# Part of a depthwise convolution moved from the Vector engine to the Scalar engine and GpSimd, in a one-core hybrid block (convolution, differential attention, mixture of experts)

## The chip, the core and the metric

The kernel runs on one NeuronCore of a Trainium2 chip, in one launch. The metric is the device time of one execution in microseconds (us). Engines are named as the profile names them: PE (matmuls), PEld (its weight loads), DVE (Vector engine), ACT (Scalar engine), POOL (GpSimd), SP (issues DMAs).

## What is computed

512 tokens of width 1024, float32. One layer: RMS norm, a projection to five groups of 512 columns (a, g, q, k, v), a convolution branch on a and g, an attention branch on q, k and v, an output projection of both, then 32 experts with the best four for each token. The branch that the change touches:

```python
def conv_mixer(a, g, conv_w, conv_b, ln_g, ln_b):
    u = a * jax.nn.sigmoid(g)
    y = lax.conv_general_dilated(u, kern, window_strides=(1,),
                                 padding=[(CONV_WIDTH - 1, 0)],      # CONV_WIDTH = 31, causal
                                 dimension_numbers=('NWC', 'WIO', 'NWC'),
                                 feature_group_count=D_CONV)        # 512 channels, one filter each
    y = layer_norm(y + conv_b, ln_g, ln_b)
    return jax.nn.silu(y)
```

The attention branch has 4 heads with two softmaxes each, `p[:, :, 0] - lam * p[:, :, 1]`, over blocks of 128 queries; `lam` is a scalar computed with two exponentials.

## The kernel before, in words

All matmuls of float32 data are done as three matmuls of a split: `hi` is the value rounded to fp32r, `lo` the rest. ACT makes `whi` of each chunk of weights, DVE makes `wlo` (`hi_front` and `lo_front` in the front part). The front part has 14 chunks of weights, numbered 0 to 13: two for each of a, g, q, k, v (0 to 9) and four of the output projection. PE takes chunk c once `lo_front(c)` is done, 48 matmuls each; `hi_front(c)` waits until PE has used chunk c - 3, because there are three `whi` buffers.

Each engine has its order of work written out by hand. DVE's, from the end of the second group (g):

1. `u_pad = a * sigmoid(g)`, signalled by `conv_in`.
2. `lo_front(6)`, 20 taps, `lo_front(7)`, 20 taps, `lo_front(8)`, 18 taps, scaling of q, `lo_front(9)`, 18 taps, `lo_front(10)`, 16 taps, scaling of k, `lo_front(11)`, four evictions of the transposed k (`kT`).
3. Three small instructions for `lam` (they wait for ACT's exponential, `lam_exp`), and then 16 attention units (4 query blocks x 4 heads). For unit i DVE takes the row maxima of unit i + 1, forms the difference `pd` of the two softmaxes of unit i, and then does 6 taps (units 0 to 4) and the remaining 2 (unit 5).

The convolution has 4 channel groups c of 128 channels, with 31 taps w each: 124 taps. A tap is one instruction on [128, 512]: it multiplies a shifted window of `u_pad` by a weight of its own for each partition and adds it to `acc`. The first tap of a group is a TENSOR_SCALAR (L849), the other 30 are SCALAR_TENSOR_TENSORs (L853). Each waits on a semaphore for the tap before it of the same group. The taps of two groups alternate (2 and 0, then 3 and 1), so that two taps in a row never depend on each other.

PE, ACT and DVE then do the layer norm between attention units: the mean is four fp32 products of `inv_dc` and `acc` (L1235), one for each channel group (group 2 in unit 3, group 0 in unit 4, groups 3 and 1 in unit 5); DVE's subtraction of the mean (`centre`, L914) follows in unit 6.

ACT in the same stretch: `hi_front(6)`, `hi_front(7)`, `hi_front(8)`, the evictions and squares of q (`qk_out(0)`, 4 evictions and 32 squares), `hi_front(9)`, `hi_front(10)`, the same for k (`qk_out(1)`), `hi_front(11)`, evictions of transposed q (`qT`, L597) and of v (`v_tok`, L600), the exponential for `lam` (L601), then the exponentials of the units. PE transposes q inside chunk 9 and k behind it (`turn_qk`, L1172); the first waits for the squares of both q and k, the second for DVE's scaled `k_tok` and for ACT's `qT`.

POOL has no work between its setup at the start and the end of attention. In the expert loop behind it POOL gathers tokens, scatters results by indirect DMA, and moves four columns of indices with four small copies per iteration (L480 to L485), while DVE subtracts `whi` from the weights (L1049) all the time.

## Time and profile before

| what | value |
|---|---|
| median of 3 runs | 1544.02 us (1540.77 to 1546.91) |
| the profiled execution's own time | 1540.77 us |
| its span in the profile | 1539.2 us |
| mean granted TensorE clock | 0.957 of full speed |
| busy: PE, DVE, ACT, POOL | 95%, 86%, 65%, 17% |

The span runs from the first to the last instruction in the trace. The front part (projections, attention, output projection, routing) lies between 0 and about 340 us; the expert loop takes the rest. The change touches the stretch from 70 to 200 us alone. A busy share over the whole span says little on that stretch, so its own rows are what to look at.

### The profile page before, as it was taken

To read this page: it belongs to the slowest core of one execution; us is meant where nothing else is said; L and a number is where in the kernel's file an instruction comes from. 1 tells how busy PE (TensorE), PEld (TensorE's weight loads), DVE (VectorE), ACT (ScalarE), POOL (GpSimd) and SP (SyncE) were. 2 spreads that over 40 slices of the span, in tenths; PEclk is the share of its full clock that TensorE was granted. 3 is DMA by queue.
4 is the path that set the end of the run, shared out by engine and by line. 5 is a ranking of instruction groups with operands and counts; after the bars stand their busy time and mean duration, and the time that the engine had idled before them with its cause. 6 is when DMAs were issued, how large, how long until landed. Compare 5 with 4: busy or idle time off the path is not lost.

```text
span 1539.2 us, 19983 instructions
## 1 busy us (share of the span) xinstructions
PE 1456.7 (95%) x6488; PEld 1160.2 (75%) x6488; DVE 1319.1 (86%) x1082; ACT 1005.0 (65%) x942; POOL 263.2 (17%) x277
## 2 busy tenths in 40 slices
PE   7996899929999999999999999999999999999996
PEld 5885457817888888888888888888888888887884
DVE  3499866547999999999999999999999999999994
ACT  5353264326777777777777777777777777777773
POOL 2000000230111221112211111122111212212121
PEclk9998589859999999999999999999999999999998
DMA  8330003677999999999999999999999999999971
GB/s 289 114 108 2 1 1 135 223 124 290 343 348 377 361 364 356 355 363 361 356 352 357 363 353 359 362 347 358 360 345 361 366 347 358 362 356 356 353 265 20
DMA packets 94743, 445.31 MB, mean 289 GB/s; under 512 B 14879, under 2 KB 14895, under 8 KB 61888
## 3 DMA queue, kind: packets, MB, share of 16 engines
q1 hardware_dynamic: 80704, 421.82, 73.9%
q0 software_dynamic: 11392, 17.61, 4.9%
q10 hardware_dynamic: 2624, 5.59, 1.4%
q8 instruction: 13, 0.21, 0.1%
q14 instruction: 10, 0.08, 0.0%
HBM read 439.56 MB, written 22.43 MB: 300 GB/s over the span
## 4 chain that ended last, share of the span: by engine, by line
PE 86%; DVE 9%; DMA 2%; issue 1%; ACT 1%; POOL 1%; ACTq 0%; POOLq 0%; DVEq 0%
PE psum L1148 25%; PE psum L1149 25%; PE psum L1150 25%; DVE acc L853 5%; PE psum L1417 2%; PE psum L1392 2%; PE psum L1401 2%; PE psum L1434 1%; PE psum L1220 1%; DVE wlo L808 1%; DMA slot_table<-payload,dest 1%; PE psum L1280 1%; POOL slot_table L441 0%; PE psum L1155 0%; PE psum L1222 0%
## 5 line engine op out<-in xcount | busy, mean ns | idle before, releaser
L1049 DVE TENSOR_TENSOR wlo<-ring,whi 128x2048 fp32r<-128x2048 f32 x384 | 876.7, 2290 | 80.6 <-ACT whi L719 77.0
L719 ACT ACTIVATE whi<-ring 128x2048 fp32r<-128x2048 f32 x384 | 737.9, 1922 | 275.4 <-PE psum L1150 275.4
L1148 PE MATMUL psum<-whi,xT_hi 128*128 128x512 f32 x1024 | 406.5, 397 | 4.0 <-DVE xT_lo L1055 4.0
L1149 PE MATMUL psum<-whi,xT_lo 128*128 128x512 f32 x1024 | 400.4, 391 | 0.0
L1150 PE MATMUL psum<-wlo,xT_hi 128*128 128x512 f32 x1024 | 400.0, 391 | 0.0
L1148 PEld LDWEIGHTS psum<-whi,xT_hi 128*128 128x128 f32 x1024 | 193.3, 189 | 53.9 <-issue 10.9
L1150 PEld LDWEIGHTS psum<-wlo,xT_hi 128*128 128x128 f32 x1024 | 193.2, 189 | 40.7
L1149 PEld LDWEIGHTS psum<-whi,xT_lo 128*128 128x128 f32 x1024 | 193.4, 189 | 38.0
L1148 PE MATMUL psum<-whi,aT_hi 128*128 128x512 f32 x512 | 202.5, 396 | 1.9 <-ACT y_sb L741 1.9
L1149 PE MATMUL psum<-whi,aT_lo 128*128 128x512 f32 x512 | 200.2, 391 | 0.0
L1150 PE MATMUL psum<-wlo,aT_hi 128*128 128x512 f32 x512 | 200.2, 391 | 0.0
L468 POOL DMA_INDIRECT out<-y_sb,slots x32 | 98.5, 3078 | 419.6 <-ACT y_sb L741 405.7
L1148 PEld LDWEIGHTS psum<-whi,aT_hi 128*128 128x128 f32 x512 | 96.6, 189 | 21.3 <-issue 2.2
L1150 PEld LDWEIGHTS psum<-wlo,aT_hi 128*128 128x128 f32 x512 | 96.5, 189 | 20.2
L1149 PEld LDWEIGHTS psum<-whi,aT_lo 128*128 128x128 f32 x512 | 96.5, 189 | 19.3
L853 DVE SCALAR_TENSOR_TENSOR acc<-u_pad,cw_sb,acc 128x512 f32<-128x512 f32 x120 | 80.5, 752 | 0.0
L480 POOL COPY slots_moved<-slots 128x4 int32<-128x4 int32 x30 | 33.6, 1121 | 273.9 <-DMA out<-y_sb,slots 273.9
L459 POOL DMA_INDIRECT xg<-hn_rows,slots x33 | 34.2, 1037 | 241.0 <-PE psum L1392 202.3
L1148 PE MATMUL psum<-whi,uT_hi 128*128 128x512 f32 x160 | 63.1, 394 | 0.8 <-DVE h L933 0.8
L1150 PE MATMUL psum<-wlo,uT_hi 128*128 128x512 f32 x160 | 62.4, 390 | 0.0
L1149 PE MATMUL psum<-whi,uT_lo 128*128 128x512 f32 x160 | 62.3, 390 | 0.0
L735 ACT ACTIVATE aT_hi<-psum 128x512 fp32r<-128x512 f32 x64 | 34.9, 596 | 40.4 <-PE psum L1401 40.4
(230 smaller groups left out, 1429.7 us busy)
## 6 DMA issues: line engine op xcount, KB each, us to landing
ring<-in_w_gate_up SPq DMA_DIRECT2D x256, 1024.0 KB, 7.7
ring<-in_w_down SPq DMA_DIRECT2D x128, 1024.0 KB, 6.9
ring<-in_w_in SPq DMA_DIRECT2D x10, 1024.0 KB, 15.0
ring<-in_w_out SPq DMA_DIRECT2D x4, 1024.0 KB, 5.2
h<-in_x SPq DMA_DIRECT2D x4, 512.0 KB, 5.5
out<-h ACTq DMA_DIRECT2D x4, 512.0 KB
hn_rows<-hn ACTq DMA_DIRECT2D x4, 512.0 KB
bias_rows<-rows_st SPq DMA_DIRECT2D x1, 1280.0 KB, 14.3
```

The lines of the kernel that those rows point to most:

```text
L459: pool.indirect_dma_start(out=xg[:, :], out_offset=None, in_=hn_rows, in_offset=bass.IndirectOffsetOnAxis(ap=slots[:, place, 0:1], axis=0) ...
L468: pool.indirect_dma_start(out=out, out_offset=bass.IndirectOffsetOnAxis(ap=slots[:, place, 0:1], axis=0), in_=y_sb[:, :], in_offset=None, ...
L480: COPY(slots_moved[:, :, token], slots[:, 1:5, token]).then_inc(move_step, 1)
L719: nc.scalar.activation(whi[:, hi_of(number), :], ring[:, slot(number), :], ACT.Copy).then_inc(hi_ready, 1)
L735: nc.scalar.activation(aT_hi[:, half * 4:half * 4 + 4, :], bank(6 + half), ACT.Copy).then_inc(aT_hi_done, 1)
L853: STT(out=acc[:, c, :], in0=u_pad[:, c, w:w + S], scalar=cw_sb[:, c, w:w + 1], in1=acc[:, c, :], op0=ALU.mult, op1=ALU.add).then_inc(conv_ ...
L1049: TT(wlo[:, slot(number), :], ring[:, slot(number), :], whi[:, hi_of(number), :].bitcast(F32), ALU.subtract).then_inc(lo_ready, 1)
L1148: MM(o, s_hi, m_hi, start=first, stop=False)
L1149: MM(o, s_lo, m_hi, start=False, stop=False)
L1150: return MM(o, s_hi, m_lo, start=False, stop=last)
L1392: ins = nc.tensor.transpose(bank(6 + half)[:, k * P:(k + 1) * P], xg[:, (half * 4 + k) * P:(half * 4 + k + 1) * P], ident[:, :])
L1401: ins = nc.tensor.transpose(bank(6 + half)[:, k * P:(k + 1) * P], act_sb[:, (half * 4 + k) * P:(half * 4 + k + 1) * P], ident[:, :])
```

## The change

`conv_tmp` is a new buffer of four [128, 512] tiles that lies in the same memory as `pd` and `pdT`. 37 of the 124 taps leave DVE: all 31 of group 3, and the last 6 of group 2. For 36 of them ACT multiplies the shifted window of `u_pad` by the weight into `conv_tmp` (`multiply`), and POOL adds the product to `acc`; the first tap of group 3 is one `tensor_scalar` on POOL. ACT may be at most four products ahead of POOL. DVE keeps 87 taps: 25 of group 2 and 31 of group 0 and of group 1. In its new order groups 2 and 0 alternate for 25 taps each, then 1 and 0 for 6, and the last 25 taps are all of group 1. Before the units DVE does 12, 12, 12, 12 and 8 taps (56, was 92), then 5 beside each of the units 0 to 4 and 6 in unit 5 (31, was 32). `pd` of unit 0 (DVE) and `pdT` of unit 0 (ACT) wait for POOL's last addition. The mean's parts are done for group 3 in unit 2, group 2 in unit 3, group 0 in unit 4, and group 1 alone in unit 5.

```diff
+        conv_tmp = at("conv_tmp", [P, 4, S], F32, up + 40960)
...
-        dve_taps = [(c, w) for pair in ((2, 0), (3, 1)) for w in range(TAPS) for c in pair]
+        SPLIT_TAP = 25
+        POOL_TAPS = [(3, w) for w in range(1, TAPS)] + [(2, w) for w in range(SPLIT_TAP, TAPS)]
+
+        dve_taps = [(c, w) for w in range(SPLIT_TAP) for c in (2, 0)]
+        rest = [(0, w) for w in range(SPLIT_TAP, TAPS)]
+        for w in range(TAPS):
+            dve_taps += [(1, w)] + rest[w:w + 1]
...
-        TAPS_BESIDE = 6
+        TAPS_BESIDE = 5
...
+            pool.wait_ge(conv_in, 1)
+            pool.wait_ge(cw_ready, 1)
+            pool.wait_ge(table_filled, 16)
+            nc.gpsimd.tensor_scalar(acc[:, 3, :], u_pad[:, 3, 0:S], cw_sb[:, 3, 0:1], cb[:, 3:4], ALU.mult,
+                                    ALU.add).then_inc(conv_pool, 1)
+            for n, (c, w) in enumerate(POOL_TAPS, 1):
+                pool.wait_ge(products, n)
+                pool.wait_ge(conv_pool, n)
+                if c == 2 and w == SPLIT_TAP:
+                    pool.wait_ge(conv_dve, 2 * SPLIT_TAP)
+                nc.gpsimd.tensor_tensor(acc[:, c, :], acc[:, c, :], conv_tmp[:, n % 4, :],
+                                        ALU.add).then_inc(conv_pool, 1)
...
+            def multiply(count):
+
+                nonlocal tap
+                for _ in range(count):
+                    tap += 1
+                    if tap == 1:
+                        act.wait_ge(conv_in, 1)
+                        act.wait_ge(bias_stored, 16)
+                    if tap > 4:
+                        act.wait_ge(conv_pool, tap - 3)
+                    c, w = POOL_TAPS[tap - 1]
+                    nc.scalar.activation(conv_tmp[:, tap % 4, :], u_pad[:, c, w:w + S], ACT.Copy,
+                                         scale=cw_sb[:, c, w:w + 1]).then_inc(products, 1)
+
             hi_front(6)
+            multiply(4)
             hi_front(7)
+            multiply(4)
...
+                    multiply(2)
...
             hi_front(9)
+            multiply(4)
             hi_front(10)
             qk_out(1, k_tok, 4, 8)
             hi_front(11)
+            multiply(2)
...
             for t in range(T):
                 nc.scalar.activation(v_tok[:, t, :], bank(t), ACT.Copy).then_inc(v_evac, 1)
+            multiply(len(POOL_TAPS) - tap)
             nc.scalar.activation(lam2[:, :], lam2[:, :], ACT.Exp).then_inc(lam_exp, 1)
...
+                if i == 0:
+                    act.wait_ge(conv_pool, len(POOL_TAPS) + 1)
...
             lo_front(6)
-            conv(20)
+            conv(12)
             lo_front(7)
-            conv(20)
+            conv(12)
             lo_front(8)
-            conv(18)
+            conv(12)
             qk_scale(0, q_tok)
             lo_front(9)
-            conv(18)
+            conv(12)
             lo_front(10)
-            conv(16)
+            conv(8)
...
                 if i == 0:
-                    dve.wait_ge(bias_stored, 16)
+                    dve.wait_ge(conv_pool, len(POOL_TAPS) + 1)
...
-                pe.wait_ge(conv_dve, dve_taps.index((c, TAPS - 1)) + 1)
-                ins = MM(bank(7), inv_dc[:, :], acc[:, c, :], start=(c == 2), stop=(c == 1))
+                if c in (2, 3):
+                    pe.wait_ge(conv_pool, len(POOL_TAPS) + 1)
+                else:
+                    pe.wait_ge(conv_dve, dve_taps.index((c, TAPS - 1)) + 1)
+                ins = MM(bank(7), inv_dc[:, :], acc[:, c, :], start=(c == 3), stop=(c == 1))
...
-            def last_means():
-                mean_part(3)
-                mean_part(1)
-
-            beside = {MEAN - 2: lambda: mean_part(2), MEAN - 1: lambda: mean_part(0), MEAN: last_means,
-                      VARIANCE: variance}
+            beside = {MEAN - 3: lambda: mean_part(3), MEAN - 2: lambda: mean_part(2), MEAN - 1: lambda: mean_part(0),
+                      MEAN: lambda: mean_part(1), VARIANCE: variance}
```

## Rows read from the trace of the kernel before

**Rows 1.** Chain that ended last, 60 to 130 us: shares, then start us, us, what.

```profile
by line: DVE acc L853 64.4%; DVE wlo L808 12.7%; PE psum L1150 3.9%; PE psum L1148 3.6%; PE psum L1149 3.6%; DVE q_tok L861 3.3%; DVE u_pad L836 2.7%; DVE acc L849 2.6%; ACT sig_g L568 2.3%; issue 1.3%; DVE qk_rstd L859 0.4%
```

**Rows 2.** Waits, 55 to 215 us: who waited for whom, total us, times, longest.

```profile
ACT whi L544 <- PE psum L1150: 30.4, 4, 9.0
PE psum L1172 <- DVE k_tok L861: 13.8, 1, 13.8
```

**Rows 3.** Timeline of DVE, 72 to 214 us: start us, us, what.

```profile
71.91 2.28 DVE L808 TENSOR_TENSOR wlo<-ring,whi 128x2048 fp32r<-128x2048 f32 x1
75.02 12.01 DVE L853 SCALAR_TENSOR_TENSOR acc<-u_pad,cw_sb,acc 128x512 f32<-128x512 f32 x18
86.95 2.29 DVE L808 TENSOR_TENSOR wlo<-ring,whi 128x2048 fp32r<-128x2048 f32 x1
...
119.13 2.29 DVE L808 TENSOR_TENSOR wlo<-ring,whi 128x2048 fp32r<-128x2048 f32 x1
...
153.12 0.06 DVE L881 MEMSET vecs<- 128x1 f32 x1
...
154.97 0.42 DVE L889 TENSOR_REDUCE att<-psum 128x2 f32<-128x256 f32 x1 [1.39 <-PE psum L1223]
...
158.26 0.28 DVE L906 TENSOR_SCALAR pd<-prob,att 128x128 f32<-128x128 f32 x1
158.58 0.35 DVE L907 SCALAR_TENSOR_TENSOR pd<-prob,att,pd 128x128 f32<-128x128 f32 x1
...
192.09 2.29 DVE L914 TENSOR_TENSOR acc<-acc,psum 128x2048 f32<-128x2048 f32 x1 [1.23 <-PE psum L1235]
```

**Rows 4.** Groups of DVE, 71.9 to 153.2 us: line, operation, count | busy us, mean ns | idle before.

```profile
L853 DVE SCALAR_TENSOR_TENSOR acc<-u_pad,cw_sb,acc 128x512 f32<-128x512 f32 x88 | 58.8, 754 | 0.0
L808 DVE TENSOR_TENSOR wlo<-ring,whi 128x2048 fp32r<-128x2048 f32 x6 | 13.7, 2290 | 0.0
L879 DVE TENSOR_SCALAR kT<-psum,vecs 128x512 f32<-128x512 f32 x4 | 2.7, 744 | 0.0
...
L849 DVE TENSOR_SCALAR acc<-u_pad,cw_sb,vecs 128x512 f32<-128x512 f32 x4 | 2.0, 542 | 0.0
```

**Rows 5.** Timeline of ACT, 119.5 to 162 us.

```profile
122.22 0.32 ACT L586 ACTIVATE qk_rstd<-qk_ss,vecs 128x32 f32<-128x32 f32 x1
...
130.60 2.43 ACT L597 ACTIVATE qT<-psum,vecs 128x512 f32<-128x512 f32 x4 [6.24 <-PE psum L1172]
134.66 2.07 ACT L600 ACTIVATE v_tok<-psum 128x512 f32<-128x512 f32 x4 [1.63 <-PE psum L1150]
136.74 1.28 ACT L601 ACT_TABLE_LOAD   x1
```

**Rows 6.** One line each, 500 to 1400 us: count, ns min/median/max, first and last start.

```profile
L480 POOL COPY slots_moved<-slots x25: 182/979/2334, 500.6 to 1379.1; 128x4 int32<-128x4 int32 x25
...
L1049 DVE TENSOR_TENSOR wlo<-ring,whi x296: 2281/2293/2329, 498.1 to 1399.1; 128x2048 fp32r<-128x2048 f32 x148
```

**Rows 7.** Timeline of POOL in the expert loop, two iterations.

```profile
574.05 2.32 POOL L480 COPY slots_moved<-slots 128x4 int32<-128x4 int32 x1 [9.47 <-DMA out<-y_sb,slots]
...
939.97 0.18 POOL L480 COPY slots_moved<-slots 128x4 int32<-128x4 int32 x1 [9.45 <-DMA out<-y_sb,slots]
940.10 2.25 POOL L481 COPY slots_moved<-slots 128x4 f32<-128x4 f32 x1
```

**Rows 8.** Timeline of DVE at the same two places.

```profile
574.03 2.29 DVE L1049 TENSOR_TENSOR wlo<-ring,whi 128x2048 fp32r<-128x2048 f32 x1 [0.43 <-ACT whi L719]
...
939.97 2.33 DVE L1049 TENSOR_TENSOR wlo<-ring,whi 128x2048 fp32r<-128x2048 f32 x1 [0.43 <-ACT whi L719]
```

**Rows 9.** Groups of POOL, whole span: operation, count | busy us, mean ns | idle before.

```profile
L446 POOL MEMSET xg<- 128x1024 f32 x1 | 1.0, 957 | 0.0
...
L381 POOL TENSOR_SCALAR_AFFINE_SELECT ident<-ident 128x128 f32<-128x128 f32 x1 | 0.3, 284 | 0.2 <-POOL tri L380 0.2
```

**Rows 10.** Chain that ended last, 0 to 400 us: the mean, behind the last taps.

```profile
188.28 3.78 PE psum L1235 x4
```

More of the change, by code:

```diff
@@ L227, in build @@
         hi_ready, lo_ready, chunk_used = sem("hi_ready"), sem("lo_ready"), sem("chunk_used")
-        a_evac, g_sig, conv_in, conv_dve = sem("a_evac"), sem("g_sig"), sem("conv_in"), sem("conv_dve")
-        cw_turned, cw_ready = sem("cw_turned"), sem("cw_ready")
+        a_evac, g_sig, conv_in, conv_dve, conv_pool = (
+            sem("a_evac"), sem("g_sig"), sem("conv_in"), sem("conv_dve"), sem("conv_pool"))
+        cw_turned, cw_ready, products = sem("cw_turned"), sem("cw_ready"), sem("products")
         qk_evac, v_evac, qk_std, qk_scaled = sem("qk_evac"), sem("v_evac"), sem("qk_std"), sem("qk_scaled")
@@ L568, in _ @@
                 nc.scalar.activation(sig_g[:, c, :], bank(4 + c), ACT.Sigmoid).then_inc(g_sig, 1)
+            tap = 0
+            def multiply(count):
[10 more added lines that the diff above has]
+                                         scale=cw_sb[:, c, w:w + 1]).then_inc(products, 1)
             hi_front(6)
+            multiply(4)
             hi_front(7)
+            multiply(4)
             def qk_out(which, tok, first_bank, used):
```

## The prediction, made before the changed kernel was run

> **What bounds the kernel now.** I read the chain of work that ended last first, in the stretch that the change touches. From 60 to 130 us taps are 64% of it and `wlo` 13%, both DVE [rows 1]. The waits say the same from the other side: PE stood 13.8 us before the transposes of k, for DVE's scaled `k_tok`, and ACT stood 30.4 us for PE before its `whi` [rows 2]. The timeline and groups of DVE show it without idle time from 71.9 to 153.1 us [rows 3, 4]. So a microsecond taken from or added to DVE's list here moves the end, until PE's projections bind: their last matmul ends at 134.6, when ACT starts on v [rows 5]. That leaves room for a gain of about 13 us before unit 0, and none for a loss.
>
> **What DVE is relieved of.** 18 taps take from 75.02 to 86.95, 0.663 us each; instructions overlap, one alone is 0.754 [rows 3, 4]. DVE has 92 taps before the units now (88 at 0.663, 4 first taps at 0.46) and 56 after (53 and 3). That takes off 35 x 0.663 + 0.46 = 23.7 us. DVE's list from 71.9 to the end of `kT` shrinks from 81.2 to 57.5 us.
>
> **The units.** 31 taps instead of 32, but the last 24 each follow the tap that they depend on. Four of these open a unit, with other work between; 20 follow directly. Where one DVE instruction waits for the one before it, the next starts 0.04 us after its end (0.28 us from 158.26, next at 158.58) [rows 3]. So such a tap costs 0.754 + 0.04 = 0.79, 0.13 more than an independent one. 31 x 0.663 + 20 x 0.13 = 23.2 against 32 x 0.663 = 21.2: +2.0 us. Behind the last tap the mean had four passes of PE in a row, 3.8 us [rows 10]; now group 1 alone is left, two passes: -1.9 us. The parts of groups 3, 2 and 0 stand in units 2 to 4, where DVE's taps are the slower side. Together 0.
>
> **What ACT gets.** 36 products. The nearest row is `qT`, also with a scale for each partition: 4 in 2.43 us, 0.6 each, 22 us in all [rows 5]. ACT's idle time for PE (30 us) takes the eight before `qk_out(0)`. The eight in q's squares move `hi_front(9)` by 5 us; DVE's `lo_front(9)`, which needs it, came 17 us behind it, at 119.1 [rows 3]. The eight in k's squares and some waits move ACT's root for k from 122.5 [rows 5] to about 129. Both cost nothing as long as DVE comes later than that. The last six stand between v and the exponential for `lam`; these end at 136.7 + 3.6 + 1.5 = 142 if POOL keeps up, and were done at about 138 before, with DVE asking at 153 [rows 3, 5]. ACT may be only four products ahead, so a slow POOL holds up ACT's `hi_front`, too.
>
> **What POOL gets, and whom it meets.** POOL runs no [128, 512] addition before, so its price and its effect on DVE have to come from other rows. The expert loop shows the effect. POOL's copies of 128x4 take 182 ns at least and 2334 ns at most, with a median of 979 [rows 6]. The long ones stand beside DVE's subtraction with two inputs in SBUF: a copy that started at 574.05 ended at 576.37, with DVE's instruction running from 574.03 to 576.32; one at 940.10 ended at 942.35, DVE's at 942.30 [rows 7, 8]. The copy waits until the DVE instruction is through. The reverse shows once: the DVE instruction that started with a copy at 939.97 took 2.33 instead of 2.29 us, and 2329 ns is the longest of 296 [rows 6 to 8]. So the two engines take turns at something, and POOL's hold counts against DVE. A tap has both its tensors in SBUF like that subtraction, and so has POOL's addition.
>
> The Trainium skill states this as a rule (SBUF — State Buffer, "SBUF: two separate sides"): DVE and GpSimd share one port pair under an exclusive lock, taken for the whole instruction, and a DVE instruction with two SBUF inputs competes for it with a GpSimd instruction that reads SBUF. The rows agree clearly for POOL's waits and, by 40 ns, for DVE's. By the rule all 36 additions stop DVE; read narrowly, the rows bear out only that POOL waits, and that reading is the rival of a gain below.
>
> How long does an addition hold DVE? From 182 ns for 4 columns (the shortest copy) to 284 ns for 128 (the affine select, one input) is 102 ns for 124 columns, 0.82 ns a column; the memset, 957 ns for 1024, bounds it at 0.93 [rows 6, 9]. 512 columns in one pass are 0.42 us, in two passes (one for each input) 0.84, in three (the write too) 1.26. Each turn costs 0.13 beside: DVE loses its overlap of 0.09, and the copy's 0.04 is the least delay seen [rows 3, 4, 8]. That makes 0.55, 0.97 or 1.39 us. I take 1.1, between two and three passes and nearer to two, because two inputs are certain and how far the write overlaps is not. POOL's first tap, with one input, takes 0.55.
>
> The Trainium skill has a price (GPSIMD Engine Reference, "Elementwise — side-by-side cycle accounting"): 4497 ns for an addition of 2048 columns. Scaled to 512, with 156 ns of it taken as fixed, an estimate is 1.24 us; with that as the hold the sum below would be 5 us more. No row here shows it.
>
> **The sum.** DVE's list becomes 57.5 + 36 x 1.1 + 0.55 = 97.7 us against 81.2: +16.5. About 2.5 us of it falls where DVE doesn't want what POOL holds (`kT` reads PSUM, 2.7 us [rows 4], and short waits). So +14 before unit 0, +0 in the units, and everything behind moves with it: the expert loop starts later and runs as before. A second effect is inside this sum: `lo_front(9)` is done at about 135 instead of 121.4, so PE starves before chunk 9. Chunk 9 took 13.3 us, from 121.4 to 134.7 [rows 3, 5], and ends at 148 to 152 now, still ahead of DVE's scaled k (about 160). If that cover is gone, up to 3 us are added. The profiled execution's own time is 1540.8 (span 1539.2, 1.6 around it), which makes 1555; the median of the three runs is 3.2 higher, so I forecast 1558.
>
> **The rivals.** *Additions run freely beside DVE (faster).* For it: POOL is empty, and DVE's own delay is seen in one row of 40 ns. Against it: that POOL waits for whole DVE instructions, so something is exclusive. Then DVE's list would end at 130, and others bind: the squares of k give the scale at 129, chunk 9 ends at 134.6, 16 transposes and `kT` end at 138, `lam`'s exponential at 142, and POOL's last additions at about 146 (v at 136.7, six products and additions of 1.2). `pd` of unit 0 comes at 146, not at 158.9 [rows 3]: -13 us, 1531. *Cheap additions, no change.* The turn is taken, but an addition holds it for less. The point where the loss turns into a gain is (23.7 + 2.0) / 36 = 0.71 us for each addition. At the lower bound of 0.55 the sum is 20.4 - 23.7 = -3 us; at 0.85 +5 less the 2.5: from -3 to +5, 1541 to 1549. *Additions that hold longer.* At 1.39 the sum is 50.6 - 23.7 = +27 less 2.5, with ACT's `hi_front` held back by the four buffers on top: +24 to +32, about 1572. In all three the new waits (of `pd` and `pdT` for POOL's last addition) are the step that shows who was last.
>
> **How the numbers follow.** Forecast (+7.7 to +22): 0.57. Holding longer than that: 0.07. Cheap: 0.18. Free: 0.18. Half a percent, 7.7 us, is about what a measurement of this kernel can tell from no change. Slower is forecast and longer holds, 0.64; same is the cheap case, 0.18; faster is the free case, 0.18. The likeliest case's own range is 1550 to 1567. The range for 8 in 10 takes in the cheap case and much of the longer one, and leaves out most of the free one: 1539 to 1576.
>
> **What would show each step.** In the profile after: taps of 0.66 us at places without POOL and pitches near 1.7 us where POOL adds; POOL's additions ending with or just behind DVE's instructions, with durations that spread from about 1 to 2 us; `kT` ending near 167 instead of 153; a stall of PE before chunk 9; the subtraction of the mean at about 206 instead of 192.1 [rows 3]; the taps of group 1 in unit 5 at a pitch of 0.79. The prediction is wrong if the taps keep their pitch of 0.66 beside POOL (then faster), or if ACT waits long for POOL and holds up `hi_front` (then slower still, and for another reason).

## The result, and the profile after

The changed kernel takes 1560.89 us (median of 4 runs, 1559.7 to 1562.07) against 1542.74 (4 runs beside it, 1540.77 to 1546.91). The ratio is 1.0107, with a 95% interval of 1.0082 to 1.0134, which is 16.5 us. It is slower, as forecast, and inside the range. The profiled execution of after has a span of 1562.6 us, some 3 us longer than the spans of its timed runs (1558.1 to 1560.4), so differences read from it are a little too large.

Four runs of each are few here. Eleven more executions of after were timed: ten took 1558.73 to 1563.54 us, one took 1548.56. In four later sets before had medians of 1539.06 to 1539.37, and none of its runs took more than 1543.38, while two of the four above did. By the medians of all of these the change costs about 21 us, still inside what was forecast as slower (+7.7 to +22). The odd execution of 1548.56 comes up again below.

The page of after: span, busy time of each engine, and the slices of POOL and of the clock.

```profile
span 1562.6 us, 20058 instructions
...
PE 1468.6 (94%) x6488; PEld 1164.7 (75%) x6488; DVE 1329.6 (85%) x1045; ACT 1026.2 (66%) x978; POOL 325.7 (21%) x314
...
POOL 2174200041011122111221221122122111221111
PEclk9997567967999999999999999999999999999998
```

A slice is 39 us: POOL's new work stands in slices 2 to 5, and slices 5 and 6 (156 to 234 us) are among the lowest of the clock. The two turn out to be the two halves of the story.

DVE's timeline from 71.6 us answers to [rows 3]; start, length, what, and in brackets what was waited for.

```profile
71.66 2.28 DVE L853 TENSOR_TENSOR wlo<-ring,whi 128x2048 fp32r<-128x2048 f32 x1
75.08 15.03 DVE L898 SCALAR_TENSOR_TENSOR acc<-u_pad,cw_sb,acc 128x512 f32<-128x512 f32 x10
...
137.52 8.03 DVE L898 SCALAR_TENSOR_TENSOR acc<-u_pad,cw_sb,acc 128x512 f32<-128x512 f32 x12
...
195.55 4.68 DVE L898 SCALAR_TENSOR_TENSOR acc<-u_pad,cw_sb,acc 128x512 f32<-128x512 f32 x6
202.40 2.29 DVE L959 TENSOR_TENSOR acc<-acc,psum 128x2048 f32<-128x2048 f32 x1 [0.19 <-PE psum L1283]
...
223.43 3.35 DVE L964 RECIPROCAL std<-std 128x512 f32<-128x512 f32 x1 [5.88 <-ACT std L672]
```

Ten taps take 15.03 us at 75.08, where 18 took 12.01 before; twelve at 137.52 take 8.03, a pitch of 0.66, because POOL is idle there. That shows in POOL's own timeline, and in the lines of POOL's additions, of ACT's products and of the taps (count, ns least/median/most).

```profile
75.03 13.21 POOL L443 TENSOR_TENSOR acc<-acc,conv_tmp 128x512 f32<-128x512 f32 x8
109.16 26.28 POOL L443 TENSOR_TENSOR acc<-acc,conv_tmp 128x512 f32<-128x512 f32 x14 [1.12 <-ACT conv_tmp L604]
154.96 10.52 POOL L443 TENSOR_TENSOR acc<-acc,conv_tmp 128x512 f32<-128x512 f32 x6 [19.51 <-ACT conv_tmp L604]
...
L898 DVE SCALAR_TENSOR_TENSOR acc<-u_pad,cw_sb,acc x84: 734/752/1789, 75.1 to 199.5; 128x512 f32<-128x512 f32 x84
L443 POOL TENSOR_TENSOR acc<-acc,conv_tmp x36: 1264/1555/3134, 75.0 to 164.2; 128x512 f32<-128x512 f32 x36
L604 ACT ACTIVATE conv_tmp<-u_pad,cw_sb x36: 704/748/777, 71.8 to 159.9; 128x512 f32<-128x512 f32 x36
```

The shortest addition takes 1264 ns, and a tap beside POOL up to 1789 instead of 754. The waits (who for whom, total, times, longest) answer to [rows 2]:

```profile
POOL acc L443 <- ACT conv_tmp L604: 26.8, 4, 19.5
ACT qT L639 <- PE psum L1217: 18.2, 1, 18.2
PE psum L1193 <- DVE wlo L853: 15.6, 1, 15.6
PE psum L1283 <- DVE acc L898: 5.6, 1, 5.6
ACT conv_tmp L604 <- POOL acc L443: 2.5, 1, 2.5
```

PE stands 15.6 us before chunk 9, as foreseen. POOL waits for ACT's products. ACT waits for POOL once, 2.5 us before the very last product at 159.87; its `hi_front(11)` was through at 128.8 by then, so POOL held up no `hi_front` of the stretch.

Where the time went, by five milestones of each profiled execution: the start of the first `kT`, of `pd` of unit 0, of the centring (`acc` minus the mean), of the reciprocal of the deviation, and of the last addition to h. Later rows are the experiments.

| kernel | kT | pd | centring | reciprocal | last h | centring to reciprocal |
|---|---|---|---|---|---|---|
| before | 150.45 | 158.26 | 192.09 | 205.38 | 291.38 | 13.3 |
| after | 158.64 | 167.79 | 202.40 | 223.43 | 313.45 | 21.0 |
| e1_pool_tiny | 135.75 | 144.97 | 179.59 | 200.26 | 289.85 | 20.7 |
| e2_pool_memset | 134.92 | 144.54 | 179.16 | 193.22 | 279.52 | 14.1 |
| e3_pool_copy | 137.65 | 145.39 | 180.02 | 200.95 | 290.88 | 20.9 |
| e4_after_warm | 158.81 | 167.66 | 202.28 | 221.88 | 308.05 | 19.6 |
| f1_alt_tail | 158.22 | 167.38 | 200.53 | 213.94 | 299.94 | 13.4 |
| f2_before_tail | 151.52 | 160.68 | 195.41 | 214.91 | 301.02 | 19.5 |
| f3_after_warm2 | 158.97 | 167.94 | 203.07 | 216.02 | 307.21 | 13.0 |
| f4_before_warm | 151.19 | 160.35 | 194.16 | 209.41 | 299.73 | 15.3 |
| g1_few_gated | 147.93 | 157.09 | 190.91 | 204.53 | 290.58 | 13.6 |
| g2_few_free | 149.82 | 158.62 | 192.43 | 206.20 | 292.33 | 13.8 |
| g3_mean_burst | 157.77 | 166.35 | 200.95 | 221.50 | 311.01 | 20.6 |
| h1_mean_wait | 158.83 | 167.68 | 204.01 | 218.16 | 304.27 | 14.2 |

After is 8.2 us late at `kT`, 9.5 at `pd`, 10.3 at the centring, 18.1 at the reciprocal and 22.1 at the last h. The convolution explains less than half of it. The rest arises behind it, over instructions that the diff leaves alone. The windows show why: us, then busy time and count of PE, PEld, DVE, ACT, POOL, then the granted clock, DMA share and GB/s. Before:

```profile
190.00:195.00 5.00, 5.00 (x15) 2.45 (x13) 3.11 (x3) 1.30 (x5) 0.00 (x0) 0.74 0.00 0
195.00:200.00 5.00, 5.00 (x20) 2.81 (x20) 2.88 (x7) 3.31 (x6) 0.00 (x0) 1.00 0.00 0
200.00:205.00 5.00, 5.00 (x18) 2.58 (x17) 1.71 (x6) 2.01 (x3) 0.00 (x0) 1.00 0.00 0
```

After:

```profile
195.00:200.00 5.00, 0.00 (x0) 0.00 (x0) 4.79 (x8) 0.52 (x3) 0.00 (x0) 0.57 0.00 0
200.00:205.00 5.00, 4.71 (x10) 2.42 (x10) 4.36 (x8) 1.29 (x5) 0.00 (x0) 0.50 0.01 2
205.00:210.00 5.00, 5.00 (x14) 3.02 (x13) 1.22 (x4) 0.87 (x2) 0.00 (x0) 0.50 0.00 0
210.00:215.00 5.00, 5.00 (x9) 2.41 (x10) 0.97 (x3) 2.44 (x5) 0.00 (x0) 0.50 0.01 2
```

From the centring to the reciprocal, before runs PE mostly at 2.4 GHz, after at 1.2 GHz (0.50) for three windows. The products on PE that both kernels have there show it: the mean (L1235, L1283; in brackets how long PE stood idle for the last tap) and the variance (L1242, L1290), eight matmuls that took 3.59 us before and take 5.98 in after. Before, then after:

```profile
188.28 3.78 PE L1235 MATMUL psum<-acc,inv_dc 128*128 128x512 f32 x4 [3.26 <-DVE acc L853]
...
199.11 3.59 PE L1242 MATMUL psum<-ln_tmp,inv_dc 128*128 128x512 f32 x8
```

```profile
200.29 2.08 PE L1283 MATMUL psum<-acc,inv_dc 128*128 128x512 f32 x2 [5.60 <-DVE acc L898]
...
214.78 5.98 PE L1290 MATMUL psum<-ln_tmp,inv_dc 128*128 128x512 f32 x8
```

The last 4 us go the same way. The split of the convolution's output (`uT_lo`) starts 18.0 us late (221.21, 239.24), the first addition to h 22.0 us late (230.05, 252.09) and the last 22.1. So the 4 us arise between the first two of these. In the windows there, with PE busy throughout, before runs at 2.4 GHz from 225 on:

```profile
220.00:225.00 5.00, 4.96 (x16) 2.88 (x15) 3.72 (x5) 4.20 (x8) 0.00 (x0) 0.67 0.00 0
225.00:230.00 5.00, 5.00 (x20) 3.26 (x21) 2.54 (x5) 1.32 (x4) 0.00 (x0) 1.00 0.00 0
```

After, in the same work, stays at 1.2 GHz until 250:

```profile
240.00:245.00 5.00, 5.00 (x14) 2.71 (x12) 4.10 (x7) 3.57 (x10) 0.00 (x0) 0.50 0.00 0
245.00:250.00 5.00, 5.00 (x10) 2.83 (x10) 1.40 (x2) 0.00 (x0) 0.00 (x0) 0.50 0.00 0
```

Of the 23.4 us between the two spans, 10.3 thus stand ahead of the centring, 11.8 between it and the last h, and 1.3 behind that.

### The profile page after: what moved, and what is told of

Same layout as the page of the kernel before. It is cut to its first block, busy times and chain, and to the rows that moved or that the text cites. A ratio compares the mean times of both kernels' runs of the same rounds, so it can differ in the third digit from the quotient of the medians.

```text
span 1562.6 us, 20058 instructions
## 1 busy us (share of the span) xinstructions
PE 1468.6 (94%) x6488; PEld 1164.7 (75%) x6488; DVE 1329.6 (85%) x1045; ACT 1026.2 (66%) x978; POOL 325.7 (21%) x314
## 4 chain that ended last, share of the span: by engine, by line
PE 86%; DVE 9%; DMA 2%; issue 1%; ACT 1%; POOL 0%; ACTq 0%; POOLq 0%
PE psum L1193 25%; PE psum L1194 24%; PE psum L1195 24%; DVE acc L898 6%; PE psum L1461 2%; PE psum L1436 2%; PE psum L1445 2%; PE psum L1265 1%; PE psum L1478 1%; DVE wlo L853 1%; DMA slot_table<-payload,dest 1%; PE psum L1324 1%; PE psum L1267 1%; PE psum L1200 0%; PE psum L1382 0%
## 5 line engine op out<-in xcount | busy, mean ns | idle before, releaser
L898 DVE SCALAR_TENSOR_TENSOR acc<-u_pad,cw_sb,acc 128x512 f32<-128x512 f32 x84 | 87.4, 1088 | 0.7
L480 POOL DMA_INDIRECT xg<-hn_rows,slots x33 | 36.1, 1093 | 242.4 <-PE psum L1436 195.3
L501 POOL COPY slots_moved<-slots 128x4 int32<-128x4 int32 x30 | 28.5, 949 | 275.6 <-DMA out<-y_sb,slots 275.6
L1193 PE MATMUL psum<-whi,uT_hi 128*128 128x512 f32 x160 | 64.6, 404 | 16.4 <-DVE wlo L853 15.6
L443 POOL TENSOR_TENSOR acc<-acc,conv_tmp 128x512 f32<-128x512 f32 x36 | 58.8, 1634 | 31.8 <-ACT conv_tmp L604 26.8
L1436 PE MATMUL psum<-ident,xg 128*128 128x128 f32 x264 | 36.9, 284 | 29.1 <-DMA xg<-hn_rows,slots 29.1
```

The source lines that it names most:

```text
L443: nc.gpsimd.tensor_tensor(acc[:, c, :], acc[:, c, :], conv_tmp[:, n % 4, :], ALU.add).then_inc(conv_pool, 1)
L480: pool.indirect_dma_start(out=xg[:, :], out_offset=None, in_=hn_rows, in_offset=bass.IndirectOffsetOnAxis(ap=slots[:, place, 0:1], axis=0) ...
L898: STT(out=acc[:, c, :], in0=u_pad[:, c, w:w + S], scalar=cw_sb[:, c, w:w + 1], in1=acc[:, c, :], op0=ALU.mult, op1=ALU.add).then_inc(conv_ ...
L1193: MM(o, s_hi, m_hi, start=first, stop=False)
L1436: ins = nc.tensor.transpose(bank(6 + half)[:, k * P:(k + 1) * P], xg[:, (half * 4 + k) * P:(half * 4 + k + 1) * P], ident[:, :])
```

## The experiments

Theory A: POOL's additions and DVE's taps take turns, because both read their operands from SBUF, the memory in which the tiles lie, and the rest of the loss is the clock behind the convolution. Theory B: POOL's additions cost DVE little, and the loss is new waits. The totals of the first three runs are not comparable with the others. Leaving part of the convolution out changes which experts the tokens choose; the expert loop stored 33 blocks instead of 32, one iteration more of some 37 us (POOL's first copy of an iteration starts at 427.71 in before, the next at 464.90). They are read by their milestones.

**e1_pool_tiny**: the same POOL instructions and waits, with four columns each.

```diff
-                nc.gpsimd.tensor_tensor(acc[:, c, :], acc[:, c, :], conv_tmp[:, n % 4, :],
+                nc.gpsimd.tensor_tensor(acc[:, c, 0:4], acc[:, c, 0:4], conv_tmp[:, n % 4, 0:4],
```

> The changed kernel, but POOL adds only 4 of the 512 columns of each product (the other columns of the products are left out of the sum); all waits, ACT's 36 products and DVE's 87 taps stay. Turn-taking (my theory): DVE's taps go back to a pitch of 0.66 us, kT ends at 137 to 141 instead of 161.4, and the start of unit 0 is bound by ACT and PE as in the rival of free additions: 13 us or more before the kernel before at that point, time 1525 to 1535. Rival, ACT's products or the order of the waits cost the time: kT ends after 150 and the time stays over 1545.

Measured: 1570.1 us, ratio 1.0186 (1.0158 to 1.0215), one iteration of the loop more, which the 1525 to 1535 us expected did not have in them. Taps at full speed:

```profile
75.98 6.70 DVE L898 SCALAR_TENSOR_TENSOR acc<-u_pad,cw_sb,acc 128x512 f32<-128x512 f32 x10
...
L443 POOL TENSOR_TENSOR acc<-acc,conv_tmp x36: 198/517/5990, 75.9 to 141.1; 128x4 f32<-128x4 f32 x36
```

`pd` of unit 0 starts at 144.97, 13.3 us ahead of before. The rival of free additions had put it at 146 and -13. So the products, the new waits and the order of the taps cost nothing; the size of POOL's additions does. Theory B falls.

**e2_pool_memset**: instead of each addition two memsets of 512 columns, which together take about an addition's time and read nothing.

```diff
-                nc.gpsimd.tensor_tensor(acc[:, c, :], acc[:, c, :], conv_tmp[:, n % 4, :],
-                                        ALU.add).then_inc(conv_pool, 1)
+                nc.gpsimd.memset(conv_tmp[:, n % 4, :], 0.0).then_inc(memsets, 1)
+                pool.wait_ge(memsets, n)
+                nc.gpsimd.memset(acc[:, c, :], 0.0).then_inc(conv_pool, 1)
```

> The changed kernel, but each addition on POOL is replaced by two memsets of 512 columns, about 1.0 us together, which write to SBUF and read nothing (the products are left out of the sum). Theory A, POOL and DVE take turns at reading: taps keep a pitch of 0.66 us beside POOL, and times are near those of the run with 4 columns (1525 to 1535). Theory B, any work of POOL on SBUF holds DVE: taps beside POOL are spread as after the change, kT ends near 157, time 1550 to 1560.

**e3_pool_copy**: a copy of the product over `acc`, one input instead of two.

```diff
-                nc.gpsimd.tensor_tensor(acc[:, c, :], acc[:, c, :], conv_tmp[:, n % 4, :],
-                                        ALU.add).then_inc(conv_pool, 1)
+                nc.gpsimd.tensor_copy(acc[:, c, :], conv_tmp[:, n % 4, :]).then_inc(conv_pool, 1)
```

> The changed kernel, but each addition on POOL is a copy of the product, with one input instead of two (the sum over taps is left out). If the hold is the time for which POOL reads and writes: 0.5 to 0.6 us for each copy instead of about 1.0, kT ends at 146 to 150, and the time is within 0.5% of the kernel before, 1537 to 1548. If each turn has a fixed price that outweighs the columns, kT stays over 155 and the time near 1556.

Measured: 1565.8 us, 1.0188 (1.015 to 1.0225), and 1571.52, 1.019 (1.0154 to 1.0225). With memsets (first fence) the taps keep their 0.66; with copies (second) ten taps take 8.84 us.

```profile
75.15 6.70 DVE L899 SCALAR_TENSOR_TENSOR acc<-u_pad,cw_sb,acc 128x512 f32<-128x512 f32 x10
...
L899 DVE SCALAR_TENSOR_TENSOR acc<-u_pad,cw_sb,acc x84: 732/747/754, 75.1 to 176.2; 128x512 f32<-128x512 f32 x84
L445 POOL MEMSET acc<- x36: 524/526/687, 75.7 to 143.9; 128x512 f32 x36
```

```profile
75.12 8.84 DVE L897 SCALAR_TENSOR_TENSOR acc<-u_pad,cw_sb,acc 128x512 f32<-128x512 f32 x10
...
L443 POOL COPY acc<-conv_tmp x36: 612/887/3493, 75.1 to 141.3; 128x512 f32<-128x512 f32 x36
```

At its own speed DVE's list takes 78.55 - 23.7 = 54.85 us from 71.9 to `kT`. After took 86.98, without a wait of DVE, so 33 POOL instructions in that stretch cost 32.1 us, 0.97 each. 30 copies, again without a wait, cost 65.96 - 54.85 = 11.1, 0.37 each (0.5 to 0.6 was expected). With memsets it took 63.2 us, of which DVE stood 7.7 idle for ACT's roots and for PE's transposes; what is left, 55.5, is the list's own time to within 0.7, so a memset costs nothing that shows. Against these 55.5 us, which have POOL's first tap in them as the other lists do, the prices are 0.98 for each of 32 additions and 0.35 for a copy. `kT` ended at 140.4 with copies, earlier than the 146 to 150 expected. Reading is what costs, and an instruction with two inputs costs more than twice one with one. The Trainium skill (SBUF — State Buffer, "SBUF: two separate sides") has a DVE instruction with two SBUF inputs compete with a GpSimd instruction that reads SBUF; these runs agree: 0.97, 0.37 and 0 us.

**e4_after_warm**: the clock. Matmuls whose result nobody reads, 12 in unit 5 and 14 in unit 8, in a bank that is overwritten later.

```diff
                     scores(i + 2)
+                if i in {5: 12, 8: 14}:
+                    pe.wait_ge(pdT_evac, i - 1)
+                    for _ in range({5: 12, 8: 14}[i]):
+                        MM(bank(4 + i % 2), ident_r[:, :], bias_hi[:, 0, :], start=True, stop=True)
                 if i in beside:
```

> The changed kernel with 12 extra matmuls (128x512, their result is not used) on PE in unit 5, while it waits for DVE's last six taps, and 14 in unit 8, while it waits for the norm. Theory, the second part of the loss is PE's clock (0.50 from 200 to 219 us in the changed kernel, 1.00 in the kernel before at the same work): the stretch from centring to the reciprocal of the deviation shrinks from 21.0 us to about 13, and the time falls by 6 to 10 us, to 1551 to 1555. Rival, that stretch is longer because of waits and not of the clock: it stays at 20 us or more and the extra matmuls add 3 to 6 us.

Measured: 1552.36 us, 1.0078 (1.0055 to 1.01); the stretch from centring to reciprocal 19.6 us, not 13. The 12 were through by 195.3, PE was idle for 4.9 us behind them, and the clock stood at 0.50 from 200 to 215. It says nothing against the clock, since it did not hold it. The time lies in the expected 1551 to 1555 all the same, but not by the expected way: the stretch did not shrink. In the profiled execution the gain on after is 1.4 us up to the reciprocal (19.6 instead of 21.0) and 3.9 behind it, where the reciprocal and the last h lie 86.2 us apart instead of 90.0.

The next four share a chip. **f1_alt_tail**: after, with groups 0 and 1 in turn at the end, so that the last taps are independent, and both parts of the mean behind them.

```diff
-        dve_taps = [(c, w) for w in range(SPLIT_TAP) for c in (2, 0)]
-        rest = [(0, w) for w in range(SPLIT_TAP, TAPS)]
-        for w in range(TAPS):
-            dve_taps += [(1, w)] + rest[w:w + 1]
+        first = [(w % 2, w // 2) for w in range(SPLIT_TAP)]
+        dve_taps = [t for w in range(SPLIT_TAP) for t in ((2, w), first[w])]
+        for w in range(12, TAPS):
+            dve_taps += [(1, w)] + ([(0, w + 1)] if w + 1 < TAPS else [])
...
-                      MEAN: lambda: mean_part(1), VARIANCE: variance}
+                      MEAN: lambda: (mean_part(0), mean_part(1)), VARIANCE: variance}
```

> The changed kernel with another order of DVE's 87 taps: groups 0 and 1 alternate to the end, so no tap follows the one that it depends on, and the means of groups 0 and 1 both stand in unit 5. If the tail (dependent taps, and one mean product in unit 5 instead of two) is what cools PE's clock: unit 5 has its last six taps in 4.0 instead of 4.7 us and a denser burst on PE behind them, the stretch from centring to the reciprocal of the deviation shrinks from 21 to 13-16 us, time 1548 to 1555. If the clock hangs on the earlier stall (before chunk 9) or on chance, the stretch stays at 20 to 22 us and the time at 1557 to 1563.

**f2_before_tail**: the reverse; before, all taps on DVE, but with after's end: group 1 alone, 25 dependent taps, five in a unit, and a thin mean.

```diff
-        dve_taps = [(c, w) for pair in ((2, 0), (3, 1)) for w in range(TAPS) for c in pair]
+        dve_taps = []
+        for w in range(TAPS):
+            dve_taps += [(2, w), (3, w), (0, w)] + ([(1, w - 25)] if w >= 25 else [])
+        dve_taps += [(1, w) for w in range(6, TAPS)]
...
-            beside = {MEAN - 2: lambda: mean_part(2), MEAN - 1: lambda: mean_part(0), MEAN: last_means,
+            beside = {MEAN - 3: lambda: mean_part(3), MEAN - 2: lambda: mean_part(2), MEAN - 1: lambda: mean_part(0),
+                      MEAN: lambda: mean_part(1),
```

> The kernel before with the changed kernel's tail alone: all 124 taps on DVE, but the last 25 all of group 1, 5 taps beside units 0 to 4 and 6 in unit 5, and the means of groups 3, 2, 0 and 1 in units 2, 3, 4 and 5. No ACT products, no POOL. Own theory: centring comes within 1 us of the kernel before (192 to 194), but PE's clock stays at 0.50 through units 6 and 7, and the stretch from centring to the reciprocal grows from 13.3 to about 20: time +6 to +10 us, about 1549 to 1553. Rival: the tail is free, time within 2 us of the kernel before.

Measured: f1 1548.2 us, 1.007 (1.0057 to 1.0083); f2 1545.4, 1.0043 (1.0019 to 1.0066), where 1549 to 1553 was expected. The first is POOL's turns without the tail, the second the tail without POOL. That their ratios add up to 1.13%, against 1.07% for the change, proves little, since f2's median mixes two outcomes and the change costs nearer 21 us. f1's window, to be read beside that of after:

```profile
200.00:205.00 5.00, 5.00 (x22) 3.10 (x20) 2.85 (x2) 1.64 (x7) 0.00 (x0) 0.87 0.00 0
205.00:210.00 5.00, 5.00 (x15) 2.46 (x15) 3.60 (x12) 2.96 (x6) 0.00 (x0) 1.00 0.00 2
```

The clock is back at 2.4 GHz by 205, and the stretch takes 13.4 us. f2 shows that the tail costs time without POOL, but not in every execution. Its 11 runs were 1547.57, 1540.78, 1553.48, 1541.32, 1550.84, 1545.4, 1541.41, 1553.42, 1539.18, 1554.14 and 1538.54: in five executions, up to 1541.41, the tail costs next to nothing, in the six others up to 15 us. Its profiled one, at 1547.57, has the long stretch, 19.5 us, and the low clock:

```profile
190.00:195.00 5.00, 1.70 (x2) 0.73 (x3) 4.72 (x11) 0.00 (x0) 0.00 (x0) 0.50 0.00 0
195.00:200.00 5.00, 5.00 (x13) 2.69 (x11) 2.50 (x2) 1.30 (x5) 0.00 (x0) 0.50 0.00 0
200.00:205.00 5.00, 5.00 (x14) 2.90 (x12) 2.19 (x6) 2.86 (x5) 0.00 (x0) 0.50 0.00 0
```

**f3_after_warm2**: e4 with more matmuls, so that they fill PE's idle time.

```diff
-                if i in {5: 12, 8: 14}:
+                if i in {5: 34, 8: 26}:
```

> The changed kernel with 34 extra matmuls on PE in unit 5 and 26 in unit 8 (the run before had 12 and 14, and PE still stood idle from 195 to 200 us and fell to 0.50). If the idle time in unit 5 is what cools the clock, it stays at 1.00 from 190 to 215 us, the stretch from centring to the reciprocal falls from 21 to 13-14 us, the time to 1545-1552. If not, the stretch stays at 19 or more and the time at 1552 to 1558.

Measured: 1553.25 us, 1.0087 (1.0072 to 1.0102). The clock stays at 1.00 from 200 on and the stretch is 13.0 us, as expected; the reciprocal comes 7.4 us earlier than in after. The extra matmuls delay PE's work behind it, so that the last h gains only 6.2, and the time misses the expected 1545 to 1552.

**f4_before_warm**: can before gain by the same means? 48 extra matmuls ahead of the transposes of k, 6 in unit 7, 20 in unit 8.

```diff
+            pe.wait_ge(qT_evac, H)
+            pe.wait_ge(bias_split, 1)
+            pe.wait_ge(cast_step, 1)
+            for _ in range(48):
+                MM(bank(4), ident_r[:, :], bias_hi[:, 0, :], start=True, stop=True)
             turn_qk(1, k_tok)
...
+                if i in {7: 6, 8: 20}:
+                    pe.wait_ge(pdT_evac, i - 1)
+                    for _ in range({7: 6, 8: 20}[i]):
+                        MM(bank(4 + i % 2), ident_r[:, :], bias_hi[:, 0, :], start=True, stop=True)
```

> The kernel before with extra matmuls whose results are not used: 48 before the transposes of k (PE is idle there from 135 to 148 us), 6 in unit 7 and 20 in unit 8. If the clock is worth what the other runs say, units 0 to 5 change little (DVE's taps bound them), and the stretch from 209 to 225 us at 0.50 goes: 3 to 6 us faster than the kernel before. If the extra matmuls only delay PE's own work, within 1 us or 1 to 3 us slower.

Measured: 1543.52 us, 1.003 (1.0021 to 1.0039): slower, a miss.

```profile
135.20 11.04 PE L1216 MATMUL psum<-bias_hi,ident_r 128*128 128x512 f32 x48
...
149.12 3.68 PE L1172 MATMUL psum<-ident,k_tok 128*128 128x128 f32 x16 [2.88 <-DVE k_tok L861]
```

They end at 146.2, PE waits 2.9 us for `k_tok`, and the clock is at 0.50 again from 150. `pd` came 2.1 us later than in before, `kT` only 0.7. The rest shows up without extra matmuls too: from `kT` to `pd` it takes 9.2 us here, in f2, in g1 and in after, and 7.8 in before's profiled execution, where the window from 150 to 155 has the clock at 0.83.

**g1_few_gated** and **g2_few_free**: before, with only four taps of group 2 moved (ACT multiplies, POOL adds). In g1 POOL waits until DVE has split chunk 11, so that its additions stand beside `kT`, which reads PSUM, the memory that PE writes to. g2 has no such wait. Beside what is shown, both make PE's mean, ACT's first `pdT` and DVE's first `pd` wait for the four.

```diff
+        FEW = 4
+        KEEP = TAPS - FEW
+        dve_taps = [(c, w) for w in range(KEEP) for c in (2, 0)]
+        for w in range(FEW):
+            dve_taps += [(0, KEEP + w), (3, w), (1, w)]
+        dve_taps += [(c, w) for w in range(FEW, TAPS) for c in (3, 1)]
...
+            pool.wait_ge(lo_ready, 12)
+            pool.wait_ge(conv_dve, 2 * KEEP)
+            for n in range(FEW):
+                pool.wait_ge(products, n + 1)
...
+                nc.gpsimd.tensor_tensor(acc[:, 2, :], acc[:, 2, :], conv_tmp[:, n, :],
+                                        ALU.add).then_inc(conv_pool, 1)
...
-            conv(16)
+            conv(12)
```

> The kernel before with 4 taps (the last of group 2) moved to ACT and POOL instead of 37; ACT makes the products behind the exponential for lam, and POOL's additions wait for lo_front(11), so that they lie beside kT (PSUM) and DVE's waits, where DVE takes nothing from two places in SBUF. DVE's other 120 taps alternate as before, the means stay in their units. If turn-taking is all that an addition costs, these four cost nothing: DVE's list is 4 x 0.66 = 2.7 us shorter, pd of unit 0 and centring come 2 to 3 us earlier, time 1 to 3 us under the kernel before. Rival, an addition costs DVE also there, or the new wait of pd comes last: 0 to +3 us.

> The same, but POOL adds as soon as it has the products, at about 139 to 144 us, beside DVE's taps before unit 0. If DVE is held 1.04 us by each addition as in the changed kernel: 4 x 1.04 - 4 x 0.66 = +1.5 us at kT, so 3 to 4 us later than with the gate, time 0 to +3 us over the kernel before. Rival, four additions hide in DVE's own pauses: like the gated kernel within 1 us.

Measured: g1 1537.29 us (11 runs, 1535.7 to 1538.13), 0.9989 (0.998 to 0.9998); g2 1540.66, 1.001 (1.0002 to 1.0019). g1:

```profile
L437 POOL TENSOR_TENSOR acc<-acc,conv_tmp x4: 1262/1264/1276, 148.1 to 152.3; 128x512 f32<-128x512 f32 x4
...
147.93 2.72 DVE L901 TENSOR_SCALAR kT<-psum,vecs 128x512 f32<-128x512 f32 x4
```

g2:

```profile
L436 POOL TENSOR_TENSOR acc<-acc,conv_tmp x4: 1263/3131/5327, 139.1 to 151.2; 128x512 f32<-128x512 f32 x4
...
135.31 8.04 DVE L874 SCALAR_TENSOR_TENSOR acc<-u_pad,cw_sb,acc 128x512 f32<-128x512 f32 x12
143.65 2.97 DVE L882 TENSOR_TENSOR k_tok<-k_tok,qk_rstd 128x2048 f32<-128x2048 f32 x1
```

By the medians the four additions cost 3.4 us less where DVE reads PSUM; in the profiled executions it is 1.9 us at `kT` and 1.7 at the last h. In g1 they hold nothing, `kT` keeps its 2.72 us, and g1 is the fastest kernel of all, though by 0.1% only, with an interval that ends just short of no change. Its `kT` comes 2.5 us earlier than in before, but `pd` and the centring only 1.2 instead of the expected 2 to 3, by the slower way from `kT` to `pd` that f4 has too. In g2 not all four held DVE for 1.04 us, as was expected. The first addition, begun at 139.15, let the taps pass and ended at 144.48. Two instructions of DVE got longer, `k_tok` by 0.68 and the `wlo` behind it by 1.07, and the other two additions ran beside `kT` and behind it. So `kT` came 0.6 us earlier than in before, where 1.5 later was expected.

**g3_mean_burst** and **h1_mean_wait**: does a dense run of PE behind the last tap bring the clock back? g3 issues both last parts of the mean together in unit 5; h1 lets both also wait for the last tap.

```diff
-MEAN - 1: lambda: mean_part(0),
-                      MEAN: lambda: mean_part(1), VARIANCE: variance}
+                      MEAN: lambda: (mean_part(0), mean_part(1)), VARIANCE: variance}
```

```diff
-                    pe.wait_ge(conv_dve, dve_taps.index((c, TAPS - 1)) + 1)
+                    pe.wait_ge(conv_dve, DVE_TAPS)
```

> The changed kernel with its order of taps, but the means of groups 0 and 1 both in unit 5, as in the run with alternating taps. It tells which half of the tail costs. If the dependent taps do (unit 5 with six of them, 4.7 us, in which PE is idle): the stretch from centring to the reciprocal stays at 19 to 21 us, time like the changed kernel, +15 to +20 us. If the thin burst of PE behind the taps does: the stretch falls to 13-15 us, time like the run with alternating taps, +9 to +12 us.

> The changed kernel's order of taps, the means of groups 0 and 1 in unit 5, and both wait for DVE's very last tap, so that PE does four mean passes in a row behind it (in the run before, group 0's two passes ran ahead of the idle time and only two stood behind it). If a dense burst of PE there is what brings the clock back: the mean ends 1 to 2 us later than in the run before, but the stretch from centring to the reciprocal falls from 20.6 us to 13-15, time +8 to +12 us against the kernel before. If the dependent taps or the idle time of 4 to 6 us in unit 5 keep the clock low whatever stands behind: the stretch stays at 19 to 21 us, time +16 to +20 us.

Measured: g3 1557.29 us, 1.0114 (1.0093 to 1.0135), in five of six runs within 5 us of after, in one 1548.62. Its trace shows that the edit did not do what it was for: group 0's part ran ahead of the idle time, and two passes were left behind the last tap.

```profile
193.11 1.91 PE L1283 MATMUL psum<-acc,inv_dc 128*128 128x512 f32 x2
...
198.83 2.08 PE L1283 MATMUL psum<-acc,inv_dc 128*128 128x512 f32 x2 [3.82 <-DVE acc L898]
```

h1: 1551.22 us, 1.008 (1.0064 to 1.0095), within the expected +8 to +12 by its median. With four passes in a row behind the last tap the centring is 1.6 us later than in after, and the clock comes back:

```profile
200.00:205.00 5.00, 4.81 (x10) 2.60 (x10) 2.96 (x8) 0.56 (x2) 0.00 (x0) 0.50 0.01 2
205.00:210.00 5.00, 5.00 (x18) 2.44 (x16) 2.58 (x5) 1.87 (x6) 0.00 (x0) 0.86 0.01 2
```

The stretch is 14.2 us, and the reciprocal comes 5.3 us earlier than in after: group 0's two passes, put off until behind the last tap, hold the centring up by 1.6 us and are more than repaid. PE stood idle ahead of them as long as in after (5.5 us), and the taps were as dependent, so these two do not by themselves keep the clock low.

## Why the prediction was right, point by point

**DVE bounds the stretch, and a relief of 23.7 us.** Right. With DVE undisturbed `kT` starts at 134.9 (e2) instead of 150.45, and DVE has 7.7 us of waits on top of it, 23.2 us in all. `pd` then moves only 13.7 us in e2 and 13.3 in e1, the limit by other engines that the prediction gave. (The 158.9 there is where before's first `pd` is through; it starts at 158.26.)

**The two engines take turns.** Right, and shown: full-size additions +32.1 us, copies +11.1, memsets and four-column additions none. The reading "only POOL waits" is refuted. The estimate of 1.24 us from the Trainium skill's price (GPSIMD Engine Reference, "Elementwise — side-by-side cycle accounting") agrees with the undisturbed 1.264. A product on ACT, forecast at 0.6 us, takes 2.54 to 2.57 for four, and neither these nor ACT's one wait for POOL held DVE up.

**The hold of an addition.** 1.1 us was forecast from bounds of 0.55 and 1.39. It measures 0.97, and 1.04 in the first ten taps (14.95 us against 6.62 alone, eight additions). That is less than the 1.26 us of an addition by itself. It is the value that the prediction worked out for two passes, but by luck in part, since the same working gives 0.55 for one pass and a copy cost 0.37. 33 x 0.13 = 4.3 us of the 5.8 between +14 and the measured +8.2 at `kT` come from here; 1.3 us are added from `kT` to `pd`, by the way that was short in before alone. 0.97 is above the break-even of 0.71, so the sign was right. The working of that 0.71 has a slip: it adds the units' +2.0, a loss, to the relief. The prediction's own sum, with the 2.5 us that DVE doesn't want and POOL's first tap, gives the same 0.71.

**The units.** +2.0 - 1.9 = 0 was forecast, +0.8 measured (10.3 less 9.5). Six dependent taps take 4.68 us, a pitch of 0.79 as worked out.

**"Everything behind moves with it ... and runs as before."** This step failed. Behind the centring after loses 7.7 us more up to the reciprocal, and 4.0 more up to the last h, in its profiled execution, because PE runs at 1.2 GHz from 200 to 215 where before had 2.4 GHz from 195, and again until 250 where before had 2.4 GHz from 225. The prediction counted the two passes that are left of the mean as a gain of 1.9 us. They came behind 5.6 us of idle PE (3.26 in before), and the clock did not rise with them, as it did with four. f3 (idle time filled), h1 (four passes) and f1 (independent taps, four passes) each bring the stretch back to 13 to 14 us. f3 is the plainest, since it adds nothing but matmuls that nobody reads. The fourteen profiles agree: the six stretches of 19.5 us and more have the clock at 0.50 to 0.55 in every window that starts within 10 us behind the centring, and the eight of at most 15.3 us have a window at 1.00 there. That the clock costs this time is shown by that. The 4.0 us up to h are seen in the rows of the clock and were not switched on and off by an edit; they stand in the four profiles with a stretch of 20.6 us or more (89.5 to 90.0 us from the reciprocal to the last h) and in no other (86.0 to 86.3, without f3 and f4, which have extra matmuls there). f2 makes the loss appear without POOL.

**The total.** +14 was forecast before unit 0 and +9.5 measured, 0 in the units and +0.8, 0 behind them and +11.8 in the profiled execution. The two errors partly cancel; 1558 was 2.9 us short. The timed runs put about the same price on the clock: f1, which has POOL's turns without the tail, is 12 us below the median of after's fifteen executions (1560.16), and so is after's own odd execution of 1548.56. That this one had the higher clock is likely by its mean granted clock (0.956; the others 0.948 to 0.953), but it has no trace. The direction rests on a right mechanism, the closeness partly on luck: with the hold right and no clock term the sum would have been about +10.

**What stays open.** The tail does not fix the clock by itself: e2 has after's tail and a stretch of 14.1, and f2 goes either way from one execution to the next, while before's 22 runs beside it stayed within 3.6 us (1538.05 to 1541.57). After, to go by its times, takes the slow way in 14 of 15. The first three experiments show both ways too, some 10 us apart: e2's profiled execution, with the short stretch, took 1559.8 us, and two of its others 1571.12 and 1571.73; e1 and e3, profiled with the long stretch, took 1570 to 1572, and 1562.11 and 1561.13 in one run each. What decides it in an execution was not found. Nor was it found why the hold of an addition with two inputs is more than twice that of a copy, and why an addition sometimes alternates with the taps and sometimes lets them pass.

## What to carry to other kernels

Before moving work from DVE to POOL, ask whether both will read SBUF at the same time: an addition that POOL makes there is paid by DVE, 0.97 us here against 0.66 for the tap that it replaces, and what stands beside PSUM reads or DVE's waits was free (four additions, g1). Then look at the end of the list: where one dependent chain is left over, the engine behind it gets its work thinly and after a pause, and the clock can cost as much as the move itself. In a total that changes by 1%, compare milestones stage by stage before giving all of it to one cause.

## What was not expected of the hardware

- Who waits depends on who is running. Where POOL and DVE start together they alternate (1.04 us for an addition). An addition that arrives inside a run of back-to-back taps can let many of them pass: one took 5.33 us in g2, while the 12 taps there took an undisturbed 8.04, and one of four columns took up to 5.99 in e1. It need not: in after the addition that starts at 94.03, inside a run of taps from 92.24 on, took 1.42.
- A POOL copy of 512 columns costs DVE 0.37 us, an addition 0.97, more than twice as much; a memset that takes 0.53 us costs nothing.
- The same program, f2, took 1538.5 to 1554.1 us; its profiled execution, with the long stretch, has the clock at 1.2 GHz from 190 to 205. After has one execution in fifteen that is 11.6 us below the median.
